# Stick-breaking attention: survival factors in an SBUF ring, one value bank drained by ScalarE, gates on GpSimd, four score groups in a row

## What is computed

```python
def stick_breaking_attention(q, k, v):
    ...
    for blk in range(S // SB_BLOCK):          # 16 blocks of 128 queries
        q0 = blk * SB_BLOCK
        L = q0 + SB_BLOCK
        z = jnp.einsum('bqhd,bkhd->bhqk', q[:, q0:L], k[:, :L]).astype(jnp.float32) * scale
        ...
        log_keep = jnp.where(causal, jax.nn.log_sigmoid(-z), 0.0)
        suffix = lax.cumsum(log_keep, axis=3, reverse=True) - log_keep
        a = jnp.where(causal, jnp.exp(jax.nn.log_sigmoid(z) + suffix), 0.0)
        outs.append(jnp.einsum('bhqk,bkhd->bqhd', a.astype(v.dtype), v[:, :L]))
```

## Time and profile before

| | us |
|---|---|
| three executions, median (lowest to highest) | 3640.78 (3635.86 to 3640.91) |
| the profiled execution's own time | 3632.74 |
| its span, first to last instruction | 3630.6 |
| stick-breaking stage, first PE work to the next stage's first | 977.1 to 1385.2 |
| sparse stage, the same | 2692.2 to 3373.7 |

### The profile page before, as it was taken

One profiled execution on the slowest core, in us unless ns is written; L12 is line 12 of the kernel. 1 busy time (PEld: TensorE's weight loads), 2 busy tenths in 40 slices (PEclk: granted clock), 3 DMA queues, 4 the chain that ended last, 5 costly groups with the idle time before them and its releaser, 6 DMA issues. The chain is left out here.

```text
span 3630.6 us, 90143 instructions
## 1 busy us (share of the span) xinstructions
PE 3319.4 (91%) x36861; PEld 2889.6 (80%) x36861; DVE 2132.6 (59%) x5023; ACT 1897.3 (52%) x3756; POOL 817.9 (23%) x900
## 2 busy tenths in 40 slices
PE   5899999989888888996997999998789999999899
PEld 5777899978777776885765898897678888888787
DVE  7100100018788984331199999997967777787332
ACT  5122211126677773221386766756468888888311
POOL 3222200001377771001101533521510000000000
PEclk9999999999899999998999999998899999999999
DMA  5333421149513214356321436425663333331432
GB/s 197 110 116 116 148 67 62 48 112 229 148 38 84 72 51 144 107 160 216 104 59 49 138 113 187 138 91 172 208 178 96 84 84 84 96 84 51 154 113 86
DMA packets 368041, 416.90 MB, mean 115 GB/s; under 512 B 51744, under 2 KB 272800, under 8 KB 366368
## 3 DMA queue, kind: packets, MB, share of 16 engines
q1 hardware_dynamic: 302880, 318.55, 30.4%
q10 hardware_dynamic: 64768, 92.81, 7.1%
HBM read 247.21 MB, written 164.10 MB: 113 GB/s over the span
## 5 line engine op out<-in xcount | busy, mean ns | idle before, releaser
L1433 PE MATMUL s_o<-s_v,s_pT 128*64 128x65 f32 (+1 forms) x13056 | 435.9, 224 | 6.5 <-issue 6.5
L230 PE MATMUL s_acc<-s_wh,s_hT 128*128 128x256 f32 (+1 forms) x1408 | 430.1, 305 | 8.6 <-ACT s_parts L658 4.6
L1433 PEld LDWEIGHTS s_o<-s_v,s_pT 128*64 128x64 f32 x13056 | 401.4, 138 | 42.9 <-issue 22.0
L232 PE MATMUL s_acc<-s_wh,s_hT 128*128 128x256 f32 (+1 forms) x1408 | 429.2, 305 | 0.0
L231 PE MATMUL s_acc<-s_wl,s_hT 128*128 128x256 f32 (+1 forms) x1408 | 429.1, 305 | 0.0
L230 PE MATMUL s_acc<-s_hT,s_wh 128*128 128x512 f32 x880 | 349.6, 397 | 55.8 <-DVE s_wl L334 25.7
L1596 ACT ACTIVATE s_probs<-s_probs,s_nmx 128x512 f32<-128x512 f32 (+3 forms) x640 | 388.7, 662 | 12.2 <-DVE s_nmx L1661 12.2
L1645 DVE CUSTOM_DVE_ANT_0 s_probs<-s_s,s_scores 128x512 f32<-128x512 f32 (+3 forms) x640 | 364.7, 607 | 10.8 <-issue 6.9
L2380 DVE TENSOR_SCALAR_CACHE_REDUCE s_scratch<-s_scores,s_thr 128x384 uint8<-128x384 f32 (+4 forms) x320 | 365.3, 1209 | 1.1
L231 PE MATMUL s_acc<-s_hT,s_wh 128*128 128x512 f32 x880 | 347.5, 395 | 0.0
L232 PE MATMUL s_acc<-s_hT,s_wl 128*128 128x512 f32 x880 | 345.7, 393 | 0.0
(11 more groups left out here) (278 smaller groups left out, 7153.7 us busy)
## 6 DMA issues: line engine op xcount, KB each, us to landing
fm<-s_parts ACTq DMA_DIRECT2D x120, 512.0 KB, 2.8
s_y<-y SPq DMA_DIRECT2D x32, 640.0 KB, 5.8
y<-s_g SPq DMA_DIRECT2D x18, 1024.0 KB, 5.9
s_q<-fm SPq DMA_DIRECT2D x32, 512.0 KB, 6.5
kc<-s_parts SPq DMA_DIRECT2D x32, 512.0 KB, 3.5
s_w<-in_o_fm SPq DMA_DIRECT2D x25, 512.0 KB, 4.5
s_w<-in_o_w_in SPq DMA_DIRECT2D x12, 1024.0 KB, 5.3
s_qh<-fm SPq DMA_DIRECT2D x42, 256.0 KB, 3.3
```

The source lines that it names most:

```text
L230: nc.tensor.matmul(out, sh, mh, start=(j == 0), stop=False)
L232: ins = nc.tensor.matmul(out, sl, mh, start=False, stop=(j == n - 1))
L1433: last = nc.tensor.matmul(o_ps[half * HD:(half + 1) * HD, 0:w], pT[half][:, x0:x0 + HD], v[:, g.u.kbs[g.a + x], vc:vc + w], start=(g.first ...
```

## The change

All of it is inside `stick_breaking`:

- the sigmoid is written to a ring of 12 SBUF tiles `kept_rows` and no longer back into its PSUM bank; the scan reads it there, a score waits only for the sigmoid (`kept`) before it overwrites a `z` bank, and a sigmoid waits for the scan 12 groups before it
- `ones` moves from SBUF to a PSUM bank of its own
- the two `o` banks become one, whose two halves are used by turns; ACT copies a finished turn's values into one of 4 SBUF tiles `ob` (`drain`), and the next turn's first feed waits for that copy (`drained`)
- the gates go from DVE to POOL, one instruction for each turn, put 4 batches (`GATE_LAG`) behind the end of the turn in POOL's queue
- `LEAD` is 12 and `SCAN_LEAD` 8, and PE's queue in a batch is turn, score, score, turn, four feeds

```diff
-    NG, LEAD, SCAN_LEAD, R, BATCH, TB = len(gs), 8, 6, 12, 4, 8
+    NG, LEAD, SCAN_LEAD, R, BATCH, TB, KR, OB, GATE_LAG = len(gs), 12, 8, 12, 4, 8, 12, 4, 4
...
-        ones = sc.sb("ones", [P, BANK])
+        kept_rows = [sc.sb(f"kept{k}", [P, BANK]) for k in range(KR)]
...
+        ones = sc.ps("ones", [P, BANK])
         t_ps = [sc.ps(f"t{k}", [P, BANK]) for k in range(2)]
-        o_ps = [sc.ps(f"o{k}", [P, BANK]) for k in range(2)]
+        o_ps = sc.ps("o", [P, BANK])
...
                     if k >= 4:
-                        pe.wait_ge(scanned, k - 2)
+                        pe.wait_ge(kept, k - 2)
...
-                    if g.first and u.turn >= 2:
-                        pe.wait_ge(out_made, made_by[u.turn - 2])
+                    if g.first and u.turn >= 1:
+                        pe.wait_ge(drained, u.turn)
...
                 for n in range(0, NG, BATCH):
-                    for a in range(n, n + BATCH, 2):
-                        turn(a)
-                        if a + LEAD < NG:
-                            score(a + LEAD)
+                    turn(n)
+                    if n + LEAD < NG:
+                        score(n + LEAD)
+                        score(n + LEAD + 2)
+                    turn(n + 2)
...
-                    nc.scalar.activation(z_ps[k % 4][:, 0:w], z_ps[k % 4][:, 0:w], ACT.Sigmoid, scale=-SCALE
+                    if k >= KR:
+                        act.wait_ge(scanned, k - KR + 1)
+                    nc.scalar.activation(kept_rows[k % KR][:, 0:w], z_ps[k % 4][:, 0:w], ACT.Sigmoid, scale=-SCALE
                                          ).then_inc(kept, 1)
...
+                def drain(n):
+                    w = len(turns[n]) * HD
+                    x0 = n % 2 * 4 * HD
+                    act.wait_ge(fed, turns[n][0].turn_end + 1)
+                    if n >= OB:
+                        act.wait_ge(out_made, made_by[n - OB])
+                    nc.scalar.copy(ob[n % OB][:, 0:w], o_ps[:, x0:x0 + w]).then_inc(drained, 1)
...
+                    copy_out(n)
+                    copy_out(n + 1)
+                    drains(n // BATCH - 2, False)
+                    keep(n + LEAD)
+                    keep(n + LEAD + 1)
+                    copy_out(n + 2)
+                    copy_out(n + 3)
+                    drains(n // BATCH - 1, True)
+                    keep(n + LEAD + 2)
+                    keep(n + LEAD + 3)
...
             def _(pool):
+                def gated(n):
+                    turn = turns[n]
+                    p, first, w = turn[0].j, min(u.b for u in turn), len(turn) // 2
+                    if n % len(TURNS) == 0:
+                        pool.wait_ge(g_in[p % 2], (p // 2 + 1) * 16)
+                    pool.wait_ge(drained, n + 1)
+                    own = gt[p % 2][:, first:first + w, :]
+                    nc.gpsimd.tensor_tensor(own, ob[n % OB][:, 0:w * P].rearrange("p (b d) -> p b d", b=w), own,
+                                            ALU.mult).then_inc(out_made, len(turn))
...
                 for k, g in enumerate(gs):
+                    if k % BATCH == 0:
+                        gates_behind(k // BATCH - GATE_LAG)
...
-                                                 data0=z_ps[k % 4][:, 0:w][:, ::-1], data1=ones[:, 0:w],
+                                                 data0=kept_rows[k % KR][:, 0:w][:, ::-1], data1=ones[:, 0:w],
...
-                def output(ui):
...
-                    outputs(n // BATCH - 2)
```

More of the change, by code:

```diff
@@ L1709, in stick_breaking @@
     assert PER_PAIR % BATCH == 0
-    ends = [u.turn_end // BATCH for u in units]
+    turns = [[u for u in units if u.turn == n] for n in range(units[-1].turn + 1)]
+    ends = [turn[0].turn_end // BATCH for turn in turns]
     freed_at = {part: 1 + max(u.end for u in units[:2 * NT] if u.b == part * GB) for part in (1, 2, 3)}
@@ L1733, in stick_breaking @@
         share = [sc.sb(f"share{k}", [P, BANK]) for k in range(R)]
-        ones = sc.sb("ones", [P, BANK])
+        kept_rows = [sc.sb(f"kept{k}", [P, BANK]) for k in range(KR)]
         left = sc.sb("left", [P, CAP])
+        ob = [sc.sb(f"ob{k}", [P, 4 * HD]) for k in range(OB)]
         pT = [sc.sb(f"pT{k}", [P, BANK]) for k in range(TB)]
         z_ps = [sc.ps(f"z{k}", [P, BANK]) for k in range(4)]
+        ones = sc.ps("ones", [P, BANK])
         t_ps = [sc.ps(f"t{k}", [P, BANK]) for k in range(2)]
-        o_ps = [sc.ps(f"o{k}", [P, BANK]) for k in range(2)]
+        o_ps = sc.ps("o", [P, BANK])
         v_in = [ahead.v_in, sc.sem("v_in1")]
@@ L1752, in stick_breaking @@
         fed = sc.sem("fed")
+        drained = sc.sem("drained")
         out_made = sc.sem("out_made")
@@ L1832, in feed @@
                     x0 = u.slot * HD
-                    feed_group(nc, o_ps[u.turn % 2][:, x0:x0 + HD], [pT[(n - u.hh + x) % TB] for x in range(2)], v[p % 2], g, HD * u.hh, fed)
+                    feed_group(nc, o_ps[:, u.turn % 2 * 4 * HD + x0:u.turn % 2 * 4 * HD + x0 + HD], [pT[(n - u.hh + x) % TB] for x in range(2)], v[p % 2], g, HD * u.hh, fed)
                 for k in range(0, LEAD, 2):
@@ L1862, in copy_out, with drains @@
                     nc.scalar.copy(pT[n % TB][:, 0:gs[n].m * P], t_ps[n % 2][:, 0:gs[n].m * P]).then_inc(taken, 1)
+                def drain(n):
[5 more added lines that the diff above has]
+                    nc.scalar.copy(ob[n % OB][:, 0:w], o_ps[:, x0:x0 + w]).then_inc(drained, 1)
+                def drains(batch, within):
+                    for n, e in enumerate(ends):
+                        if e == batch and within == (turns[n][0].turn_end % BATCH != BATCH - 1):
+                            drain(n)
                 for k in range(LEAD):
@@ L1866, in _, with gates_behind @@
                 for n in range(0, NG, BATCH):
[L1867 to L1871, removed]
+                    copy_out(n)
[8 more added lines that the diff above has]
+                    keep(n + LEAD + 3)
+                drains(NG // BATCH - 2, False)
+                drains(NG // BATCH - 1, True)
+                drains(NG // BATCH - 1, False)
             @block.gpsimd
             def _(pool):
+                def gated(n):
[7 more added lines that the diff above has]
+                                            ALU.mult).then_inc(out_made, len(turn))
+                def gates_behind(batch):
+                    for n, e in enumerate(ends):
+                        if e == batch:
+                            gated(n)
                 for k, g in enumerate(gs):
+                    if k % BATCH == 0:
+                        gates_behind(k // BATCH - GATE_LAG)
                     w = g.m * P - g.first
@@ L1883, in _ @@
                                             left[:, col[k]:col[k] + w], ALU.subtract).then_inc(broken, 1)
+                for batch in range(NG // BATCH - GATE_LAG, NG // BATCH):
+                    gates_behind(batch)
             @block.vector
```

2 lines of the change are left out of this document (removed).

## The result

The changed kernel takes 3590.43 us (median of 4 runs, 3581.07 to 3600.91) against 3638.32 us (4 runs, 3634.24 to 3640.91). The ratio is 0.9874, with a 95% interval of 0.9856 to 0.9892. It is faster by 1.3%, 47.9 us; the forecast was 3598, 42.8 us less.

The account below looks back on a forecast made before the run. Bound: handing groups round a ring, DVE its busiest engine. PE's need 350 + 5 for turn ends + 5 for coupling = 360 us instead of 403.9; with +1.1 at the end, 3640.8 - 42.8 = 3598 us; 3586 to 3628 holds 8 in 10.

Parts of the forecast that it names:

- 320 groups at the sparse stage's price are 338.1 us: PE in the stick-breaking stage: at the sparse stage's 1.057 us a group, its main need is 338.1 us.
- The tail: From the last feed to the next stage's first PE work: +1.1 us, the gate going over ACT and POOL.
- the ring through the banks: Score, sigmoid, scan, share, turn through four z banks: cutting it removes DVE's 31.7 us and PE's 9.6 us of waits.
- With a lead of 12 groups ... what was made too late now is made in time: Shares for PE: three batches of lead instead of two remove PE's 42.1 us of waits nearly whole.
- Between the two turns of a batch now stand two scores, longer than ACT's two copies, which is most of PE's 28.1 us: PE's queue: two scores outlast ACT's copies (1.18 us), removing most of PE's 28.1 us of waits for copies.
- I take the scan as unchanged: DVE's scans: swapping which operand is in PSUM and which in SBUF costs nothing; they stay at 335 us.
- Nothing to pay: ACT's sigmoid into SBUF instead of PSUM: no extra time, from 589 ns against 591 ns for a copy to SBUF.
- POOL's pace: Rival, chance 0.17: POOL needs 356 us if the 0.135 us between shares is its own; stage 364 to 370 us.
- PE standing at every turn's end: Rival, chance 0.10: ACT drains late, PE waits up to 1 us more at 40 turns; gain 3 to 25 us.
- The rival of perfect overlap: Rival, chance 0.07: the four engines overlap perfectly; stage 345 to 350 us, whole time 3582 to 3587 us.
- turn, copy and turn remain the ring that counts: Rival, chance 0.04: between PE and ACT, only DVE's 20 us change hands; time stays at 3634 to 3647 us.
- The slower rival: Rival, chance 0.07: scans suffer from their new operands; if DVE's and POOL's SBUF reads exclude each other, +260 us, 3900.

Follow-up runs that it names:

- e5: Changed kernel with the scores' lead at 8 groups instead of 12 (scan lead 6): 3586.6 us, ratio 0.9868 to the kernel before, stage 354.3 us.
- e9: The changed kernel run again, nothing altered: 3589.4 us, ratio 0.9871 to the kernel before, stage 361.1 us.
- e3: Changed kernel with PE's old queue order, turn and score alternating, lead 12 kept: 3625.7 us, ratio 0.9974 to the kernel before, stage 399.5 us.
- e1: Changed kernel, but a score again waits for the scan of its bank, not its sigmoid: 3692.5 us, ratio 1.0156 to the kernel before.
- e7: Changed kernel with no score between a batch's two turns: 3687.4 us, ratio 1.0140 to the kernel before, stage 456.1 us.
- e2: Changed kernel with the ones in SBUF, so the scan has two SBUF inputs: 3779.5 us, ratio 1.0405 to the kernel before.
- e4: Kernel before plus only ACT's drains and POOL's gates, DVE's outputs removed: 3644.0 us, ratio 1.0025 to the kernel before, stage 407.8 us.

## Why the prediction was right

The number was right above all because of the price it started from. "320 groups at the sparse stage's price are 338.1 us" was read from a stage that already had two scores between its turns, and the sum of 360 us met 363.2 and 361.1. The tail was given as +1.1 us and is +0.6, the drains at turns inside a batch as 0.6 us each, 8 times; they are 8 times, at most 0.5 us.

How close it came is in part luck. PE was busy 345.2 us, not 350, the 8.2 us for the mask were weight loads, which run beside matmuls, and the 5 us for imperfect overlap had no row. Against that stand the stops and the lower clock, some 8.5 us that no term has: without most of them the same order gives 354.3 us (e5). And 3598 was the change of -42.8 us put on a median of 3640.8; against 3638.3 us the change is -47.9, and in e9 -46.0.

The attribution behind the number was largely wrong.

- "So the 31.7 us of DVE and the 9.6 us of PE go", as the first effect of cutting the ring through the banks: with the ring cut and the old order (e3) 4.4 us are gained, and DVE waits 49.5 us for sigmoids. After the change it still waits 20.5. These were largely waits of engines that had time. What the release does is to allow the order: without it the order costs 60 us over before (e1). What the release is worth alone was not run.
- "With a lead of 12 groups ... what was made too late now is made in time": false. A lead of 8 gives the same 8.8 us of waits for shares (e5), and a lead of 12 under the old order still has 36.2 (e3). The 42.1 us were misread as well: they are waits of PE's loads, not of its matmuls. In the kernel before, 78 of 80 second turns start with the end of the copies, and outside that stretch PE's matmuls stood only 7.1 us.
- "Between the two turns of a batch now stand two scores, longer than ACT's two copies, which is most of PE's 28.1 us": the right mechanism, under-sized. It is 36.3 us (e3), and e7 shows the same chain with no score in it. PE stood 40.1 us in it before, not 28.1. The sign that the prediction gave for its ring, waits for shares under 10 us, came true through this chain.
- "I take the scan as unchanged": right, 1265 and 1260 ns. The reason given, that an operand's place makes no difference, held only because one input stayed in PSUM; with both in SBUF it is 1818 (e2).
- "Nothing to pay" for the sigmoid into SBUF: off by 34 ns at 512 columns. The Trainium skill's rule (ScalarE: Activation LUTs, "Step-by-step: what each stage is for") had the direction right. It was hidden: ACT has 299.8 us to do.

Of the rivals, POOL's pace falls: its pitch is 0.99 us, so the 0.135 us between shares was DVE's. PE standing at every turn's end falls: 8 waits, not 48. The rival of perfect overlap was priced without the +1.1 us of the tail, so 3583 to 3588; the stage stayed 13 us above its 350. The rival "turn, copy and turn remain the ring that counts" had the right ring: it was the one that counted before, and e3 and e4 are kernels in which it stays. The change takes most of it away by its order. The slower rival was a real hazard that this change steps around.

## What to carry to other kernels

Where two engines hand two buffers back and forth (turn, copy, turn), look at what the waiting engine's own queue has to do between the two halves; moving one call there was worth 36 us, once the banks came free early enough for it, and a longer lead nothing. Idle time that an engine has beside a chain it doesn't set is not a gain to be had: DVE's 20 us of gate products came off and the stage got no shorter. The waits of one engine's loads and matmuls, added up line by line, don't say which wait ends last: cut the time at the starts of the two turns and count the engine's idle time in each part. A nearby stage of the same kernel that already runs the same functions in the other order is a better price than the sum of the waits.

## What the hardware showed unexpectedly

- A tensor scan with both inputs in SBUF and a two-input instruction on POOL lengthen each other: at 512 columns the scan goes from 1.26 to 1.82 us and the share from 1.04 to 1.69, and at 127 columns the share from 399 to 1098 ns (e2 against the changed kernel). With one of the scan's inputs in PSUM, whichever of the two, the share stays at 1036 ns.
- After the stop of 2.9 us PE's granted clock was 0.74 over the next 10 us window, and 0.83 in the repeat; the stop of 2.2 us left it at 1.00, its repeat of 2.0 us fell in a window of 0.83. By the estimate above the lower clock cost about as much again as the longer stop.
